# Square sums between groups of conditioning tiles, and the last two expert blocks kept on chip while the other rows are gathered

## The reference, cut to what matters

```python
def rmsnorm(x, w):
    xf = x.astype(jnp.float32)
    y = xf * lax.rsqrt(jnp.mean(xf * xf, axis=-1, keepdims=True) + RMS_EPS)
    return y.astype(x.dtype) * w
...
    h = rmsnorm(x, norm1_w) * (1.0 + scale1) + shift1
...
    return (jax.nn.silu(xe @ w_gate[e]) * (xe @ w_up[e])) @ w_down[e]   # one block of rows of one expert
...
    y_slot = yb[dest] * wts.reshape(-1)[order][:, None].astype(x.dtype)
    return jax.ops.segment_sum(y_slot, tok, num_segments=n_tok)
...
    x = x + gate2 * ffn.reshape(bsz, L, D_MODEL)
...
    y_prompt = rmsnorm(xp, norm_f_w)
```

## Time and profile before

| | us |
|---|---|
| median of 3 runs | 1599.13 |
| lowest and highest | 1597.62, 1607.71 |
| the profiled execution | 1600.05 |
| its span in the profile | 1598.1 |
| PE, DVE, ACT, POOL busy in the span | 1439.1, 520.1, 310.3, 123.1 |

### The profile page before, as it was taken

How to read it: one execution, slowest core, us unless ns; L and a number is a source line. 1 busy time by engine, 2 the same in 40 slices (tenths; PEclk the granted TensorE clock), 3 DMA queues, 4 the chain that set the end, 5 groups by cost and what they waited for, 6 DMA issues and landing times.

```text
span 1598.1 us, 46446 instructions
## 1 busy us (share of the span) xinstructions
PE 1439.1 (90%) x20350; PEld 1081.6 (68%) x20351; DVE 520.1 (33%) x1101; ACT 310.3 (19%) x523; POOL 123.1 (8%) x194
## 2 busy tenths in 40 slices
PE   4999999887878999999991899999999999999994
PEld 2698787666767766666460778768867767768762
DVE  4893822737777231211436001101101110101114
ACT  2204023522222610000110111111111111111112
POOL 0050423000000000000002000000000000000002
PEclk9999999889999999999995899999999999999997
DMA  9278523341220011140119890890894999899975
GB/s 369 79 200 328 93 66 80 142 164 68 69 91 26 14 66 53 66 197 14 65 63 366 320 378 20 306 370 20 324 355 176 394 345 402 337 364 379 347 289 200
DMA packets 87895, 319.73 MB, mean 200 GB/s; under 512 B 11520, under 2 KB 11648, under 8 KB 87584
## 3 DMA queue, kind: packets, MB, share of 16 engines
q1 hardware_dynamic: 72288, 270.05, 44.2%
q0 software_dynamic: 13152, 41.00, 8.7%
q10 hardware_dynamic: 2400, 7.87, 1.8%
HBM read 283.72 MB, written 33.06 MB: 198 GB/s over the span
## 4 chain that ended last, share of the span: by engine, by line
PE 73%; DMA 10%; DVE 7%; SPq 4%; ACT 3%; issue 2%; POOL 1%; POOLq 0%; DVEq 0%; ACTq 0%
PE ps L1928 20%; PE ps L1522 10%; PE ps L1915 10%; PE ps L1510 9%; DMA expert_w<-in_w_down 7%; PE ps L1833 4%; PE ps L1869 4%; SPq L501 4%; PE ps L1778 3%; PE ps L1608 2%; DMA weight_ring<-in_stream 2%; PE ps L1691 1%; PE ps L1702 1%; PE ps L1898 1%; PE ps L1588 1%
## 5 line engine op out<-in xcount | busy, mean ns | idle before, releaser
L1928 PEld LDWEIGHTS ps<-x_block_t,expert_w 128*64 128x64 f32 x14336 | 427.9, 139 | 40.1 <-issue 37.2
L1928 PE MATMUL ps<-x_block_t,expert_w 128*64 128x64 f32 x14336 | 432.4, 223 | 18.8 <-DMA expert_w<-in_w_up 9.7
L1915 PE MATMUL ps<-expert_w,act_t 128*64 128x512 f32 x896 | 209.4, 598 | 4.4 <-DMA expert_w<-in_w_down 4.0
L1455 DVE TENSOR_TENSOR act_t<-silu_tmp,ps 128x64 f32<-128x64 f32 x224 | 49.5, 221 | 401.3 <-ACT silu_tmp L869 401.3
L1522 PE MATMUL ps<-h_t,weight_ring 128*128 128x320 f32 x640 | 176.7, 432 | 0.0
L1522 PEld LDWEIGHTS ps<-h_t,weight_ring 128*128 128x128 f32 x640 | 120.7, 190 | 52.6 <-issue 5.7
L1510 PE MATMUL ps<-h_t,weight_ring 128*128 128x320 f32 x512 | 150.8, 458 | 3.6 <-ACT h_t L652 3.6
L1510 PEld LDWEIGHTS ps<-h_t,weight_ring 128*128 128x128 f32 x512 | 102.8, 203 | 47.7 <-issue 11.1
L1915 PEld LDWEIGHTS ps<-expert_w,act_t 128*64 128x64 f32 x896 | 58.0, 136 | 109.8 <-issue 107.5
L869 ACT ACTIVATE silu_tmp<-ps 128x64 f32<-128x64 f32 x224 | 50.0, 223 | 414.8 <-PE ps L1928 414.8
L1778 PE MATMUL ps<-node_x 128*128 128x128 f32 x560 | 74.0, 291 | 30.2 <-DVE att L1223 16.0
(11 more groups left out here) (323 smaller groups left out, 1350.0 us busy)
## 6 DMA issues: line engine op xcount, KB each, us to landing
expert_w<-in_w_gate SPq DMA_DIRECT2D x128, 512.0 KB, 9.7
expert_w<-in_w_up SPq DMA_DIRECT2D x128, 512.0 KB, 11.6
expert_w<-in_w_down SPq DMA_DIRECT2D x128, 512.0 KB, 15.2
weight_ring<-in_stream SPq DMA_DIRECT2D x98, 512.0 KB, 4.7
x_sorted<-zero POOLq DMA_DIRECT2D x18, 512.0 KB, 14.3
x_block<-x_sorted ACTq DMA_DIRECT2D x30, 256.0 KB, 6.1
y_sorted<-y_block POOLq DMA_DIRECT2D x56, 128.0 KB, 5.5
y_sorted<-zero POOLq DMA_DIRECT2D x9, 512.0 KB, 25.3
```

Of the source, the lines that this page charges most:

```text
L1455: vec.tensor_tensor(act_t[:, f, :], silu[:, f % 2, :], ps[:, 2 + f % 2, 0:MB], ALU.mult)\
L1915: last = mm(ps[MB * half:MB * half + MB, 4, :], act_t[:, f, :], w_slot[3 * f + 2][:, 4 * half:4 * half + 4, :].rearrange("p k c -> p (k c) ...
L1928: last = mm(ps[cols, 2 * w + f % 2, 0:MB], w_slot[3 * f + w][:, k, cols], x_blk_t[:, k, :], start=(k == 0), stop=(k == KD - 1))
```

## The change

Four things. (1) At the start PE adds up the squares in two halves, behind the first and behind the second group of conditioning tiles. (2) The root and the reciprocal become `exp(-0.5 * ln(...))` on ACT, ahead of the copy of the third group; DVE's reciprocal goes. (3) The last two blocks aren't stored to DRAM. DVE multiplies their result by the gate into `y_last` (a copy for the latent tokens' gate and one for the prompt's, each in two operations of 64 rows), and two selection matrices `pick`, built and turned ahead of the expert loop, place the 64 rows at their tokens, weighted, by matmul. POOL loops over two blocks fewer and gathers the rows of all other blocks while the last two run; the rows of `y_sorted` that belong to the last two are zero (one more 512 KB zeroing DMA, placed in POOL's queue ahead of the expert stage). The gathers go to four buffers instead of ten, so columns 2 to 4 wait for `got_used`. DVE weights the gathered rows and adds them to `x2`: 20 parts (4 per column), of which 6 stand behind block 26's products, 8 beside and 6 behind block 27's. (4) In the end DVE does one addition per column where it did a multiplication and an addition, and ACT loads the table for `Sqrt` ahead of the columns.

```diff
--- before.py
+++ after.py
@@ -204,7 +204,8 @@
         h2_t = [at(f"h2_t{c}", ring0 + 12288 + 4096 * c if c < 3 else pool0 + 16384 + 4096 * (c - 3), [P, KD, P])
                 for c in range(CH)]
         zero = at("zero", end, [P, 512])
-        w_diag = at("weight_diag", ring0 + 16384, [P, 2 * CH, P])
+        pick = at("last_tokens", ring0 + 12288, [P, 2, CH, 2, MB])
+        pick_t = at("last_tokens_t", ring0 + 17408, [P, 2, CH, P])
         ada_rows = at("ada_rows", end, [P, GRP * P])
         assert base + end + 2048 <= nc.sbuf_usable_end
@@ -417,7 +425,7 @@
 
         STEPS = [(d, l) for d in range(2) for l in range(LEVELS)]
 
-        RAW1 = (A["ada1a"], A["ada1a"] + 1, A["ada1a"] + 2, A["ada1b"])
+        RAW1 = (A["ada1a"], A["ada1a"] + 1, A["ada1b"], A["ada1b"] + 1)
@@ -519,7 +527,8 @@
                                   kc[r * 32:r * 32 + GC, :, lo:lo + P]).then_inc(loaded, 16)
 
 
-        ZEROED = 16 * ((X_ROWS + P - 1) // P + (OVER * MB + P - 1) // P - 2)
+        Y_ZERO = (EXPERTS - 2) * MB
+        ZEROED = 16 * ((X_ROWS + P - 1) // P + (Y_ROWS - Y_ZERO + P - 1) // P - 2)
@@ -592,9 +601,9 @@
             pool.wait_ge(route_ready, 1)
 
             pool.sem_inc(y_copied, 1)
-            blocks = pool.value_load(rint[0:1, TOTAL:TOTAL + 1], min_val=EXPERTS, max_val=NBLK)
+            stored = pool.value_load(rint[0:1, LAST2:LAST2 + 1], min_val=EXPERTS - 2, max_val=NBLK - 2)
             with pool.Fori(0, NBLK) as i:
-                with pool.If(i < blocks):
+                with pool.If(i < stored):
 
...
-            pool.wait_ge(y_stored, blocks * 32 + 32)
+            pool.wait_ge(y_stored, stored * 32 + 32)
...
             for c in range(CH):
+                if c >= 2:
+                    pool.wait_ge(got_used, c - 1)
                 for j in range(2):
-                    pool.indirect_dma_start(out=got[2 * c + j][:, :], out_offset=None, in_=y_sorted,
+                    pool.indirect_dma_start(out=got[2 * (c % 2) + j][:, :], out_offset=None, in_=y_sorted,
                                             in_offset=bass.IndirectOffsetOnAxis(ap=dest(c, j), axis=0))\
                         .then_inc(got_in[c], 16)
...
+            act.wait_ge(const_in, 16)
+            act.wait_ge(for_act, A["ss1"] + 1)
+            nc.scalar.activation(rms[:, :, :], pair(A["ss1"]), ACT.Ln, scale=1.0 / D, bias=eps).then_inc(rms_log, 1)
+            act.wait_ge(rms_log, 1)
+            nc.scalar.activation(rms[:, :, :], rms[:, :, :], ACT.Exp, scale=-0.5).then_inc(rms_ready, 1)
+            act.wait_ge(rms_ready, 1)
+            act.sem_inc(act_took, 1)
             take_rows(RAW1[2], ada_rows1[2], GRP)
-            act.wait_ge(const_in, 16)
-            take(A["ss1"], rms[:, :, :], ACT.Sqrt, scale=1.0 / D, bias=eps)
             take_rows(RAW1[3], ada_rows1[3], GRP)
...
+            nc.scalar.activation(rms2[:, 32:33], eps, ACT.Sqrt)
...
-            dve.wait_ge(act_took, A["ss1"] + 1)
-            done(vec.reciprocal(rms[:, :, :], rms[:, :, :]))
             vectors(V["ada1"], 0, 16)
...
+            dve.wait_ge(rms_ready, 1)
...
+            note(vec.tensor_scalar(rint[:, LAST2:LAST2 + 1], ob[:, 0:1], -2.0, None, ALU.add))
+            done(vec.tensor_scalar(rt[:, N_D5, 10:11], ob[:, 0:1], float(-MB), float(2 * MB), ALU.mult, ALU.add))
...
-            vec.tensor_tensor(w_diag[:, :, :], bc(ident, 1, 2 * CH), bc(rt[:, N_GS, 20:30], 2, P), ALU.mult)\
-                .then_inc(w_diag_ready, 1)
-            blocks = dve.value_load(rint[0:1, TOTAL:TOTAL + 1], min_val=EXPERTS, max_val=NBLK)
+            done(vec.tensor_tensor(rt[:, N_A, 0:10], rt[:, N_D5, 0:10],
+                                   rt[:, N_D5, 10:11].broadcast_to((P, 10)), ALU.add))
+            done(vec.tensor_scalar(rt[:, N_A, 10:20], rt[:, N_A, 0:10], float(-MB), None, ALU.add))
...
+            for u in range(2):
+                note(vec.tensor_tensor(hit1, slots, bc(rt[:, N_A, 10 * u:10 * u + 5], 2, MB), ALU.is_equal))
+                done(vec.tensor_tensor(hit2, slots, bc(rt[:, N_A, 10 * u + 5:10 * u + 10], 2, MB), ALU.is_equal))
+                note(vec.tensor_tensor(hit1, hit1, bc(rt[:, N_GS, 20:25], 2, MB), ALU.mult))
+                done(vec.tensor_tensor(hit2, hit2, bc(rt[:, N_GS, 25:30], 2, MB), ALU.mult))
+                note(vec.tensor_tensor(pick[:, u, :, 0, :], hit1, hit2, ALU.add))
+                done(vec.tensor_tensor(pick[:, u, :, 1, :], hit1, hit2, ALU.add))
+            vec.nop().then_inc(pick_ready, 1)
...
+            last2 = dve.value_load(rint[0:1, LAST2:LAST2 + 1], min_val=EXPERTS - 2, max_val=NBLK - 2)
+            dve.wait_ge(pick_turned, 1)
+            turned = pick_t[:, :, :, :].rearrange("p u c t -> p (u c t)")
+            vec.tensor_copy(turned[:, 0:512], ps[:, 7, :])
+            vec.tensor_copy(turned[:, 512:1024], ps[:, 5, :])
+            vec.tensor_copy(turned[:, 1024:1280], ps[:, 4, 0:256]).then_inc(pick_taken, 1)
+
...
+            def add_gathered(n):
+
+                c, part = n // 4, n % 4
+                cv = 0 if c < SCH else 1
+                j = part % 2
+                row = got[2 * (c % 2) + j]
+                if part == 0:
+                    dve.wait_ge(got_in[c], 32)
+                if part < 2:
+                    note(vec.scalar_tensor_tensor(row[:, :], row[:, :], rt[:, N_GS, 20 + 5 * j + c:21 + 5 * j + c],
+                                                  g2_row[:, cv, :], ALU.mult, ALU.mult))
+                    return
+                settle()
+                note(vec.tensor_tensor(x2[:, c, :], x2[:, c, :], row[:, :], ALU.add))
+                if part == 3:
+                    settle()
+                    vec.nop().then_inc(got_used, 1)
+
+            def take_last(u, cv):
+
+                for half in range(2):
+                    rows = slice(MB * half, MB * half + MB)
+                    last = vec.tensor_tensor(y_last[rows, u, cv, :], ps[rows, 4, :],
+                                             g2_row[rows, cv, 512 * half:512 * half + 512], ALU.mult)
+                last.then_inc(y_last_ready, 1)
...
-                with dve.If(i < blocks):
+                with dve.If(i < last2):
...
+            added = [0]
+            for u, (beside, behind) in enumerate(((0, 6), (8, 6))):
+                for f in range(KF):
+                    dve.wait_ge(silu_ready, last2 * KF + (u * KF + f + 1))
+                    vec.tensor_tensor(act_t[:, f, :], silu[:, f % 2, :], ps[:, 2 + f % 2, 0:MB], ALU.mult)\
+                        .then_inc(prod_ready, 1)
+                    if f < beside:
+                        add_gathered(added[0])
+                        added[0] += 1
+                for _ in range(behind):
+                    add_gathered(added[0])
+                    added[0] += 1
+                dve.wait_ge(down_done, last2 * KF + (u * KF + KF))
+                take_last(u, 0)
+                take_last(u, 1)
+                dve.wait_ge(y_last_ready, 2 * u + 2)
+                vec.nop().then_inc(y_copied, 1)
+
             for c in range(CH):
-                cv = 0 if c < SCH else 1
                 dve.wait_ge(summed, c + 1)
                 vec.tensor_tensor(fin[c][:, :].rearrange("p (a n) -> p a n", a=2), ps[:, 2 * (c % 2):2 * (c % 2) + 2, :],
-                                  g2_row[:, cv, :].rearrange("p (a n) -> p a n", a=2), ALU.mult).then_inc(sum_took, 1)
-                dve.wait_ge(sum_took, c + 1)
-                vec.tensor_tensor(fin[c][:, :], fin[c][:, :], x2[:, c, :], ALU.add).then_inc(x3_ready, 1)
+                                  x2[:, c, :].rearrange("p (a n) -> p a n", a=2), ALU.add).then_inc(x3_ready, 1)
...
-            for i in range(3):
-                ada(RAW1[i], T_ADA1 + GRP * i, GRP)
-
+            def square_sums(k0, k1):
+                for k in range(k0, k1):
+                    for a in range(2):
+                        last = mm(pair(A["ss1"])[:, a, :], ones, x_sq[:, k, a * HALF:(a + 1) * HALF], start=(k == 0),
+                                  stop=(k == KD - 1))
+                        if k == k0 and a == 0:
+                            first(last)
+                return last
+
+            ada(RAW1[0], T_ADA1, GRP)
             act_bank(A["ss1"])
             pe.wait_ge(const_in, 16)
             pe.wait_ge(sq_ready, 1)
-            for k in range(KD):
-                for a in range(2):
-                    last = mm(pair(A["ss1"])[:, a, :], ones, x_sq[:, k, a * HALF:(a + 1) * HALF], start=(k == 0),
-                              stop=(k == KD - 1))
-                    if k == 0 and a == 0:
-                        first(last)
-            last.then_inc(for_act, 1)
+            square_sums(0, KD // 2)
+            ada(RAW1[1], T_ADA1 + GRP, GRP)
+            square_sums(KD // 2, KD).then_inc(for_act, 1)
+            ada(RAW1[2], T_ADA1 + GRP * 2, GRP)
             ada(RAW1[3], T_ADA1 + GRP * 3, GRP)
...
+            pe.wait_ge(pick_ready, 1)
+            for n in range(2 * CH):
```

(25 more changed lines are left out.)

29 lines of the change are left out of this document (19 added, 10 removed).

## The result

Over five executions each, the changed kernel takes 1587.49 us (median) against 1604.44 of the kernel before: ratio 0.9917, 95% interval 0.9889 to 0.9946, so about 13 us faster. (The ratio is estimated from the single executions; the two medians alone lie 17 us apart.) Forecast were 1576.0, a range of 1569 to 1587 and, at 0.85, a gain of over 1%: the direction was right, the size not; of a gain of 23 us, 10 did not come.

A forecast was written before the change was run, and what follows sets the result against it. It took chains at start and end to matter, PE and weight transfers bounding the kernel between. Sum: 1598.1 - 7.1 + 0 - 17.3 = 1573.7, with 1.95 outside the span 1575.7, rounded to 1576; range 1569 to 1587.

The forecast's parts named there:

- Start, -7.1: Kernel start: with the square sums moved earlier, x is scaled from 43.8 instead of 50.9; bounds -1.6 and -8.
- they arrive at 38 and 39: Start: conditioning tiles 14 and 15, reloaded behind tiles 8 and 9, land at 38 and 39; fourth group ends at 39.5.
- rival B: Start: the ring of tiles starves and the fourth group comes 5.5 us later than worked out; time 1581.2, chance 0.10.
- The loop's start, 0: Start of the expert loop: the new selection work ends at 880.1, covered by 0.8 us; bounds 0 and +1.5.
- DVE's empty passes, +2.7: Block 26: nine passes of 0.69 delay DVE's first product, for which PE's third slice waits; bounds 0 and +3.5.
- g = 8.2: Blocks 26 and 27: time from `got_used` to both gathers of a column landed, taken as 8.2 beside weights.
- Block 27 ends at 1557.5 to 1558.7: End: the last `down` tile lands at about 1557.5, ten gathers included, so block 27 ends then, below 1561.0.
- PE's empty passes end by 1560.6, about when the parts end: End: passes end 1.9 behind the last block, so block 26's sums for columns 0 and 1 are nearly done.
- Columns: Final five columns: DVE bounds them, 17.1 us from its first addition at 1563.7 to the end at 1580.8.
- rival A: Columns: matmul halves don't overlap, so PE bounds them at 3.5 per column; time 1578.4, chance 0.14.
- rival E: End: gathers are queued behind the weights with g = 12; time 1582.7, chance 0.12.
- D: End: gathers queued behind the weights make the kernel slower than before; g = 26.6 gives 1611.9; chance 0.04.

The follow-up runs named there:

- spread: Changed kernel with one of the eight square-sum pairs behind each of tiles 4 to 11, third group's rows ahead of Ln and Exp: 1587.30 us, 0.9904 of kernel before.
- loops_if: Changed kernel with all four loops ending by a register at their own last block, test kept in every pass: 1582.38 us, 0.9887 of the kernel before.
- pe_loop: Changed kernel with only PE's block loop ending at the number of blocks, without empty passes or test: 1586.50 us, 0.9897 of the kernel before.

## Why the prediction was wrong, step by step

- **Start, -7.1: mis-sized, it measured -1.6 at the first projection and nothing in the total.** Where the sums stand and ACT's Ln and Exp were right. The step that failed is "they arrive at 38 and 39": I worked out single slots of the ring and overlooked that a first half of 6.7 us lets all tiles in flight land, so that the transfers stop (35 GB/s). The last tile's transfer was issued at 35.58 instead of 34, took 5.88 us instead of the 5 up to 39, behind the tiles held up before it, and came at 41.5. That is rival B's mechanism at half its price: the group's end was 2.7 late, not 5.5. The other 3.0 is "the turning takes 3.73 as before": PE had waited, and got 1.2 GHz. spread shows both by taking both away. That the 1.6 would be gone before the experts, 1.3 of it by 208 us and the rest in the stretch with the falling clock, was in no case of mine.
- **The loop's start, 0: right, down to the 0.8 us of cover.** DVE's last new copy ends at 882.17 and PE waits for the block's rows until 883.10:

```profile
881.76 0.41 DVE L1485 COPY last_tokens_t<-ps 128x256 f32<-128x256 f32 x1
883.10 1.09 PE L1979 MATMUL ps<-constants,x_block 64*128 64x64 f32 x8 [2.59 <-DMA x_block<-x_sorted]
```

- **DVE's empty passes, +2.7: too large.** The nine passes stand in the chain of waits at 0.53 each, from 1512.1 to 1516.9, not at 0.69; DVE's first product came 5.1 behind the copy, and PE waited 1.01. The mechanism is confirmed by loops_if, where the passes and the wait are gone.
- **g = 8.2: too small.** From POOL's release to both gathers landed it was 12.0 for column 2 (1534.3 to 1546.3), just at the bound that I had set for the forecast, 10.3 and 10.4 for columns 3 and 4. DVE's parts ended 54.9 behind the copy instead of 52.1, and 1.0 instead of 3.5 behind block 27. The wait spread to PE, since DVE works in order: 1.87 us in block 27. POOL took 1.92 and 1.79 for two of the ten gathers instead of 0.94, each time while DVE scaled with two SBUF inputs. The port rule of the Trainium skill ("SBUF — State Buffer", "SBUF: two separate sides") agrees with these two; they are 0.9 us each. The other eight were issued while DVE did nothing or read PSUM, so the rule had nothing to hold there, and it does not come twice in every column, as I had assumed. (My g of 9.3 did not follow from twice 1.3 us either, which added to 8.2 is 10.8.)
- **"Block 27 ends at 1557.5 to 1558.7": mis-sized, and through PE's passes it set the end.** Relative to the copy that is 48.6 to 49.8; it measured 53.95. The last weights came 52.9 behind the copy instead of 48.6. Of these 4.3 us, 1.5 is the order: I let the last gathers be the last to land, and they overtook the weights (column 4's landed at 1561.96, the last weights at about 1564.9). The other 2.8 is the sum of the transfers, 50.1 forecast and 52.9 measured; 0.9 of it is a slip, since 1546.3 and 13.6 make 1559.9 and not 1559. `down` waited 3.9 us for weights where I had allowed 1.5. Without gathers block 27 ends at 47.15.
- **"PE's empty passes end by 1560.6, about when the parts end": mis-sized.** 51.7 behind the copy forecast, 58.2 measured (1570.2): 4.2 from the block's end (53.95 against 49.8), and 2.3 because the passes no longer ran ahead of the matmuls (4.2 behind the block's end instead of 1.9). Behind it, column 0's addition came 5.15 after PE's start instead of about 1: 2 of that are block 26's eight matmuls, which I had taken as done by then and which take 1.99 at full clock (loops_if), and 2 are the clock. Together DVE's first addition was 8.7 late (63.49 against 54.8), which is the whole loss of the end. An estimate splits it: in pe_loop and loops_if the first addition comes 2.96 behind the start of `y_last`, so DVE's own chain alone would have put it at 58.05 here. So 3.3 of the 8.7 are the gathers' g, and 5.4 came by PE's passes and its clock.
- **Columns: right.** 16.5 us from the first addition to the end against 17.1, DVE's last columns 2.5 apart, and at full clock a column's matmuls took 1.99, where 3.5 stood for no overlap: the halves of 64 rows overlap, and rival A is out. What I quoted from the Trainium skill's page "TensorEngine Tiling (Array Packing)" stands there under "Key Properties"; the trace agrees with these 1.99 us.

Rival B's mechanism and rival E's together with PE's passes and the clock make up the miss; D, the slower case, stayed far off. To a change of under 1%, which is what came, I had given 0.12; and the chances of the cases that I counted as faster by over 1% add up to 0.90, not 0.85.

## What to carry to other kernels

Work that is moved into a stream of transfers must be cut finer than what the buffers in flight can bridge, or it stops the stream and, with PE idle behind it, costs the clock too. The empty passes of a loop with a fixed count and a test inside came onto the critical path here once work for the last blocks followed them on DVE and PE; ending the loops by a register, with the body unchanged, took about 6 us off the end. Transfers that are overlapped with the last weights don't cost nothing: those weights are what the last block waits for, and engines that work in order pass the wait on.
